# A new set of costs for the block that is spread beside the second half's experts

## The reference

```python
def swiglu(h, w_gate, w_up, w_down):
    return (jax.nn.silu(h @ w_gate) * (h @ w_up)) @ w_down
...
    for layer in range(DEPTH_2):
        x = x + mixers[layer](rms_norm(x, mix_norms[layer]))
        xn, mn, wq, wkv, wo = xattn[layer]
        x = x + memory_cross_attention(rms_norm(x, xn), rms_norm(mem, mn), wq, wkv, wo)
        fn, wg, wu, wd = ffns[layer]
        x = x + swiglu(rms_norm(x, fn), wg, wu, wd)
    return rms_norm(x, final_norm)
```

## Time and profile before

| | |
|---|---|
| median of 3 runs | 4411.25 us (4410.53 to 4413.61) |
| the profiled execution | 4403.51 us, its span 4401.7 us |
| mean granted TensorE clock | 0.872 |
| busy share of the span: PE, DVE, ACT, POOL | 80%, 50%, 16%, 31% |
| read from HBM | 830.80 MB, 189 GB/s over the span |

### The profile page before, as it was taken

How to read it: one execution, slowest core, us unless ns; L and a number is a source line. 1 busy time by engine, 2 the same in 40 slices (tenths; PEclk the granted TensorE clock), 3 DMA queues, 4 the chain that set the end, 5 groups by cost and what they waited for, 6 DMA issues and landing times. The chain is left out here.

```text
span 4401.7 us, 39387 instructions
## 1 busy us (share of the span) xinstructions
PE 3531.9 (80%) x14422; PEld 2564.4 (58%) x14422; DVE 2222.3 (50%) x4375; ACT 710.1 (16%) x1574; POOL 1379.7 (31%) x1215
## 2 busy tenths in 40 slices
PE   7888988887666666664777998779867889999898
PEld 3456467875222332432556776567755668877687
DVE  2443234446777667667767667777643320132201
ACT  2211222212111111111222001210012210021100
POOL 0640012212666556464434555445500000000000
PEclk9887998998888888887768999789978789997999
DMA  6410300014888778797758999779931124421243
GB/s 190 111 61 19 89 15 1 1 50 156 312 320 300 265 277 317 256 335 285 259 174 290 394 394 344 267 266 381 394 123 56 39 86 153 134 86 39 96 153 105
DMA packets 444022, 835.58 MB, mean 190 GB/s; under 512 B 46579, under 2 KB 286255, under 8 KB 443823
## 3 DMA queue, kind: packets, MB, share of 16 engines
q0 software_dynamic: 147456, 536.94, 33.6%
q1 hardware_dynamic: 296374, 296.13, 21.1%
HBM read 830.80 MB, written 2.17 MB: 189 GB/s over the span
## 5 line engine op out<-in xcount | busy, mean ns | idle before, releaser
L2624 PE MATMUL banks<-arena 128*128 128x256 f32 (+1 forms) x4992 | 1164.9, 393 | 90.4 <-DVE arena L2694 44.6
L2624 PEld LDWEIGHTS banks<-arena 128*128 128x128 f32 (+1 forms) x4992 | 979.9, 198 | 268.2 <-issue 69.4
L2206 POOL DMA_INDIRECT arena<-in_peer_v,arena x512 | 589.8, 1152 | 636.2 <-DVE arena L2316 297.3
L2330 DVE CUSTOM_DVE_ANT_0 arena<-arena 128x1024 f32<-128x1024 f32 x512 | 628.2, 1227 | 202.3 <-DMA arena<-in_peer_u,arena 184.3
L2206 POOL DMA_INDIRECT arena<-in_peer_u,arena x512 | 568.9, 1111 | 481.6 <-DVE arena L2330 242.9
L2274 PE MATMUL banks<-arena 128*128 128x512 f32 x768 | 442.3, 717 | 275.9 <-ACT arena L2292 164.9
L2274 PEld LDWEIGHTS banks<-arena 128*128 128x128 f32 x768 | 163.3, 227 | 519.9 <-issue 324.4
L2316 DVE SCALAR_TENSOR_TENSOR arena<-arena 128x1024 f32<-128x1024 f32 x316 | 406.2, 1286 | 32.3 <-DMA arena<-in_peer_v,arena 17.5
L3390 PE MATMUL banks<-arena 128*128 128x256 f32 x1408 | 310.4, 378 | 0.0
L3432 DVE TENSOR_TENSOR arena<-banks,arena 128x512 f32<-128x512 f32 x44 | 30.4, 692 | 532.0 <-PE banks L2624 531.3
L3390 PEld LDWEIGHTS banks<-arena 128*128 128x128 f32 x1408 | 265.7, 189 | 38.3
(11 more groups left out here) (325 smaller groups left out, 4108.8 us busy)
## 6 DMA issues: line engine op xcount, KB each, us to landing
arena<-in_l_w_gate SPq DMA_DIRECT2D x44, 1024.0 KB
arena<-in_l_w_up SPq DMA_DIRECT2D x44, 1024.0 KB
arena<-in_l_w_down SPq DMA_DIRECT2D x44, 1024.0 KB
arena<-in_ada_w SPq DMA_DIRECT2D x24, 1024.0 KB, 8.4
arena<-in_l_w_qkv SPq DMA_DIRECT2D x24, 1024.0 KB
arena<-in_w_in SPq DMA_DIRECT2D x36, 512.0 KB
arena<-in_l_w_out SPq DMA_DIRECT2D x16, 1024.0 KB
arena<-in_peer_q_w SPq DMA_DIRECT2D x20, 512.0 KB
```

The lines of the kernel that those rows point to most:

```text
L2206: p.e.indirect_dma_start(e.ring[slot], None, tables[table], bass.IndirectOffsetOnAxis(ap=e.IDX[h][:, t, j:j + 1], axis=0)).then_inc(*p.up( ...
L2330: p.e.tensor_tensor_reduce(out=e.prod, in0=e.ring[slot], in1=e.H2[:, t, :], scale=1.0, scalar=0.0, op0=ALU.mult, op1=ALU.add, accum_out=e. ...
L2624: ins = p.e.matmul(out, left(c), right(c), start=c == 0, stop=c == c_n - 1, skip_group_check=True)
```

## The change

Product matmuls get a cost of their own, `WM` = 320 in place of 427; the 427 stays for the small matmuls. The cost of a unit gets 900 more. The list of costs that the block yields is thus another, and its sum too; what each engine issues is the same.

```diff
-MM = 427
+MM, WM = 427, 320
@@ product_pe, product_pause
-            yield MM * (c % group + 1)
+            yield WM * (c % group + 1)
@@ unit_cost
-    return unit.m * 5 + 300
+    return unit.m * 5 + 1200
@@ ffn_pe
                 if o % 4 == 3:
-                    yield 4 * MM
+                    yield 4 * WM
```

## The result

The changed kernel takes 4424.28 us (median of 8 runs, 4419.11 to 4435.42) against 4410.73 us for the kernel before (8 runs, 4405.87 to 4413.61): the ratio is 1.0034, 95% interval 1.0024 to 1.0045, so it is 13.5 us slower. The forecast was 4423, slower by 11.2. Its profiled execution took 4422.36 us, span 4420.4.

What follows compares the result with a forecast made beforehand. DMA was taken to bound the feed-forward stages, TensorE the other products, the loop through VectorE the attention units. Costs of 67.7 us against 56.5 us given back made +11.2, said as 4423 us; 8-in-10 range 4396 to 4441.

Steps and rivals of the forecast that it cites:

- FFNs give back: Two feed-forward stages, bound by DMA, lose expert steps: first 265 to 238 us (-27), second 269 to 241 us (-28).
- expected leftover waits: First feed-forward stage: 2 to 3 us of waits remain where the data and TensorE limits meet.
- Rival 3: Both feed-forward stages: weights stay late, only 32.5 of 65 us come back; +34, 4445 us; chance 0.08, within slower.
- Even units: Even attention units: 11.9 more steps, 23.8 expert operations at 1.2 us each, +28.6 us.
- Cross units: Two cross-attention unit stages: 5.6 more steps, 11.2 operations at 1.3 us, all second in their gap, +14.6 us.
- Dilated units: Dilated attention units: 7.5 more steps, 15 expert operations at 1.1 us each, +16.5 us.
- rival 4: Dilated attention units: more VectorE work thins out TensorE's, half clock lasts longer; +10 us, 4433; chance 0.06, within slower.
- Borders: Gelu table loads after each 16 steps: three newly fall among attention units, 2 us each, +6 us (0 to 10).
- Product stages: Product stages other than feed-forward, bound by TensorE: 6.1 steps moved away give back only 1.5 us (0 to 4).
- scale stages: Eight scale stages: 1.6 more steps together, 3.2 expert operations at 0.6 us, +2 us.
- Sum: Whole kernel: 67.7 us of costs against 56.5 us given back, +11.2 us, said as 4423 us.
- Rival 1: Attention units: operations overlap, 0.6 us each gives 4379 us, 0.8 us gives 4400; decides from 0.83 downward; chance 0.27, faster.

## Why the prediction was right, point by point

The marks that the prediction named for being right were all met: the FFNs at 242 and 240 us with L2316 56 times in each, the even, cross and dilated units at 183, 40 and 208.5 us, and the Gelus of steps 48, 64 and 192 among the units.

- **FFNs give back.** Forecast 27 and 28, measured 22.4 and 28.4. The mechanism (data) is shown by the half weights. The prediction's 263 us at 393 GB/s was no test of it, as the 393 was read from the same stage. The expected leftover waits of 2 to 3 us were a little more in the first; at 61 steps they were 8.5 us over the data's 251 us. Near the point where data and TensorE meet, the first FFN took 3.3 to 9.5 us over the larger of the two in the plans that were run. Rival 3 was this, with its price too high. The Trainium skill's 425 GB/s ("DMA: Bandwidth & Descriptors", Bandwidth) was reached in none of the FFN windows of any run: the highest over a whole FFN is 393 in the earlier trace rows, at a share of 1.04. It was by that figure that the sum held.
- **Even units.** Forecast +28.6, measured +23.9: 1.0 us per operation instead of 1.2. Of the 29 gaps, 10 had been empty and got their first operation, and 7 got a second; the other added operations lie elsewhere in the stage. The price near the upper end was too high for that mixture.
- **Cross units.** Forecast +14.6, measured +16.7; the second operation of a gap at 1.26 us is shown in the timeline. The price was right and the count was short: the traces have 7 and 6 operations between the first scale and the last before, 13 and 13 after, which is 13 more and not 11.2, at 1.28 us each.
- **Dilated units.** Forecast +16.5, measured +22.0. The step that failed is the count: I charged 15 added operations and left those that were there in place. In fact 320 for a projection's matmul and 900 more for a unit also took 6.9 operations away from beside the projections, where the slope above gives them no cost, and put 21.9 more at unit costs. The slope is a fit, but the two prices of the gaps, read elsewhere, give the growth without a term for the clock (210.1 us, above). The clock, rival 4, stands beside this: 0.81 instead of 0.85, and 7.5 us more of TensorE's time. Whether the lower clock is a cause or only follows from the thinner work is not shown; with half-width operations the changed plan's dilated units have a clock of 0.85 again.
- **Borders.** Forecast +6, measured nothing (0.3 us between the two losses). This term failed as a mechanism: the row with TensorE waiting behind the Gelu showed who released it, not that the wait would have gone without the table loads, and it did not go (2.87 us). The Trainium skill's 2.66 us for a switch ("ScalarE: Activation LUTs", What ACT_TABLE_LOAD costs) is not borne out by the earlier trace rows, where the Gelu begins 1.29 us after its load. On the path of the block not even the row's 1.28 us could be seen.
- **Product stages.** Forecast -1.5, measured -1.0 for the seven together; the output product at 30.9 both times: bound by TensorE, as said. The scale stages: forecast +2, measured +2.2 together, though each moved by up to 1.2 us.
- **Sum.** Forecast +11.2, measured +13.1 in the block and +13.5 in the medians. The errors of the single terms (-4.6 even, +5.5 dilated, -6 borders, +2.1 cross, +4.1 FFNs, and +0.8 for the rest) cancelled for the most part. That the total came this near is luck: the terms missed by 23 us if no sign is counted.
- **Rival 1** (operations overlap in the units, faster) needed under 0.83 us per operation; the unit stages showed 1.0 to 1.5. With operations of half the width the changed plan was the faster one.

## What to carry to other kernels

When background work is spread over a stage list by costs, price a step by what it adds where it lands, not by how long the stage is: here it is data in one stage, a serial loop through one engine in another, and nothing in a third. Giving the loop-bound stage a larger cost sends it exactly the work that lengthens its loop; take steps only from stages that are bound by what the step needs, and give them to places where the loop's engines have other work to cover them. The plans that did the first half of this gained 0.2 to 0.4%. A change that moves a cost also moves the work within a stage, so count the operations per gap, not per stage: here the first one in a gap cost 0.85 us, the second 1.26, and one beside a projection next to nothing.

## What the hardware showed that was not expected

Some executions lose about 20 us long before the block. The profiled execution of the changed kernel without Gelus started its block at 2074.8 us, the changed kernel's at 2054.9. Up to about 155 us it ran level with the kernel before; then equal code, 876 and 875 matmul records, took 282 us instead of 260, at a granted clock of 0.76 instead of 0.85 (windows of the same columns; before first):

```profile
155.00:415.00 260.00, 217.50 (x876) 135.34 (x876) 110.86 (x254) 53.24 (x144) 78.39 (x27) 0.85 0.18 51
```

```profile
155.00:437.00 282.00, 239.57 (x875) 150.68 (x875) 110.53 (x252) 53.15 (x144) 77.53 (x27) 0.76 0.16 47
```

The 22 us are TensorE's: it was busy 239.57 us instead of 217.50. A stretch inside, again with before first:

```profile
340.00:390.00 50.00, 44.39 (x216) 29.88 (x214) 19.26 (x59) 13.11 (x34) 0.00 (x0) 0.91 0.04 11
```

```profile
340.00:390.00 50.00, 44.89 (x168) 28.68 (x167) 16.53 (x48) 10.14 (x27) 0.00 (x0) 0.74 0.04 11
```

TensorE was busy 44 of 50 us in both; at the lower clock it got through 168 matmul records instead of 216. The products-only profile and the half-width one on the plan of before have the same (0.74, with 171 and 174 records), and they too start their block late, at 2077.6 and 2074.2 us. The other profiles stand at 0.86 to 0.91 in this stretch. What sets the clock lower in one execution and not in another stays open. This is why single profiles are read here from the block's start to its end.
